# A transformer pair on one core: some chunk pairs of two down projections multiplied with seven block products in place of eight

## The chip, the cores and the metric

The kernel runs on one core of one Trainium2 chip. The metric is device microseconds of one execution. TensorE (PE in the rows, its weight loads PEld) multiplies; VectorE (DVE) and ScalarE (ACT) do everything elementwise; SyncE (SP) issues nearly all transfers.

## The reference

Two blocks are applied to 256 tokens of 2048 features, all in fp32. The first has a convolution branch and an attention branch, then a feed-forward layer; the second has block attention with pooling, then a gated convolutional feed-forward layer. What the change touches are the two down projections:

```python
    u = jnp.square(jax.nn.relu(jnp.einsum('bsd,df->bsf', h, w_ff1[l])))
    x = x + jnp.einsum('bsf,fd->bsd', u, w_ff2[l])
...
    gate, val = jnp.split(y, 2, axis=-1)
    return (jax.nn.silu(gate) * val) @ w_down
```

w_ff2 is 8192 x 2048, w_down 5632 x 2048. Between them stand the final norm of the first block and the projection w_in_2 of the second.

## The kernel before

**Precision.** Each fp32 factor is split into a high part, a copy in the matmul's fp32r format, and a low part, the rest. A product is three matmuls: high by high, high by low, low by high.

**Weights.** All weights come in tiles of 512 KB: two chunks (128 rows each) by 512 columns, called units in the code. SyncE loads them in one fixed order into five buffers RAW (`load_to`). For each, ScalarE copies the high part into WH and VectorE subtracts it for the low part in WL (`split_to`); I call this a split, and its place in WH and WL, of which there are five, a slot. RAW's buffer is free when WL is made, and then the load five further on goes out. A slot is free when TensorE is through with it. The code asks for the split of tile u+4 when TensorE's matmuls of tile u have been written down:

```python
                hl_free[u] = t
                split_to(u + AHEAD)
                pump()
                pump()
```

**The order.** Each engine's instructions are written down once, by a Python program, and then run in that order. An item is one output block of 512 columns (for 16 chunks: eight tiles). `take` gives it four of the eight PSUM banks, the two halves in turn. When its matmuls are written, its evacuation, a generator, goes into a list (`later`), and each `pump` after a tile of the next item writes down one more step of it. So the evacuation of an item stands on VectorE and ScalarE between the splits of the next one. `side` gives, within an item, the half of the banks that the item itself doesn't hold, and makes TensorE wait until they are free:

```python
            s = turn[0]
            while free[s] is None:
                assert pending
                pump()
            PE.wait([free[s]])
            free[s] = None
```

`V.step` makes a VectorE operation wait for the one ahead of it; `V.do` doesn't.

**The stages that matter.** The first feed-forward layer runs in four parts (`seg` in the code; here parts 0 to 3): four items of w_ff1 (`feature_item`, 22.3 us each) make 16 chunks of u in MHL, then four items of w_ff2 (`token_item`) multiply these 16 chunks by the part's rows and add into XT, two banks an item. The evacuation of a w_ff1 item (`ff_evac`) is: a copy TA from PSUM, an addition from PSUM, a product with RB, the relu-square, and a split into MHL. In part 3 each w_ff2 item has a longer evacuation (`final_evac`): the addition into XT, squares on ScalarE, the scaling by GF, squares again; and `turn_x_item` turns the finished quarter of x back into XHL (eight small matmuls into the side banks, then ScalarE and VectorE split them), for items 0 to 2 during the next item's sixth tile, for item 3 in the first w_in_2 item. The second feed-forward layer has three parts with 12, 16 and 16 chunks (`SEGS`). A part has gate and value items of w_up, whose evacuations (`gate2_evac`, `val2_evac`) apply a convolution with eight tap operations on VectorE, and then four w_down items. The item ahead of w_down is a gate item of the next part, except in the last part, where it is a value item, whose evacuation ends with a split into MHL.

## Time and profile before

| | us |
|---|---|
| median of 3 runs | 2402.22 (2401.73 to 2403.05) |
| the profiled execution, its own time | 2401.66 |
| its span, first to last instruction | 2399.9 |
| TensorE busy | 2392.3 |
| VectorE busy | 1515.0 |
| ScalarE busy | 1168.0 |

The span is what the profiler sees of the execution; the time has 1.8 us around it. A busy TensorE is a queue of matmuls that overlap: the length of one in a row (0.39 us) is longer than the distance from one to the next, so distances count.

### The profile page before, as it was taken

Reading aid. Unit: us, or ns where it says so; the run is one execution under the profiler, and the core shown is the slowest. Engines: PE = TensorE matmul, PEld = TensorE weight load, DVE = VectorE, ACT = ScalarE, POOL = GpSimd, SP = SyncE. Lnnn points to the kernel's source line nnn. Section 1 sums busy time; section 2 is a strip of 40 time slices with the busy share of each in tenths; the row PEclk is TensorE's granted clock in tenths of the full one; section 3 lists DMA queues with packets and bytes.
Section 4 is the critical chain, followed back from the end, with each engine's and each line's share of the span. In section 5 each row is a group of like instructions: output and inputs, shape, how many; then the busy total and the mean of one; then the engine's idle time right before and its main releaser. Section 6 shows DMA issues by size and latency. Waiting matters only on the chain.

```text
span 2399.9 us, 30366 instructions
## 1 busy us (share of the span) xinstructions
PE 2392.3 (100%) x12653; PEld 2048.4 (85%) x12653; DVE 1515.0 (63%) x1536; ACT 1168.0 (49%) x1353; POOL 0.2 (0%) x4
## 2 busy tenths in 40 slices
PE   9999999999999999999999999999999999999999
PEld 8788888888888888888888888888888888888887
DVE  6575656666566466566556667855777577756774
ACT  5454454455444344344344555555555455535552
POOL 0000000000000000000000000000000000000000
PEclk9999999999999999999999999999999999999999
DMA  7556556565556665665655565555565665566564
GB/s 251 160 178 197 165 189 196 193 188 197 186 177 203 194 220 193 194 191 190 194 188 182 188 186 164 167 183 185 185 185 196 189 192 177 202 193 187 181 208 143
DMA packets 238037, 452.13 MB, mean 188 GB/s; under 512 B 16569, under 2 KB 20779, under 8 KB 237771
## 3 DMA queue, kind: packets, MB, share of 16 engines
q1 hardware_dynamic: 237147, 449.07, 58.7%
q8 instruction: 99, 1.62, 0.3%
q10 hardware_dynamic: 752, 1.12, 0.1%
q14 instruction: 39, 0.32, 0.0%
HBM read 446.46 MB, written 3.67 MB: 188 GB/s over the span
## 4 chain that ended last, share of the span: by engine, by line
PE 99%; DVE 1%; ACT 0%; DMA 0%; issue 0%; ACTq 0%; DVEq 0%
PE PS L71 99%; DVE WL L71 0%; DMA VR<-in_g_mix 0%; DVE PB L71 0%; DVE TA L71 0%; ACT TA L71 0%; ACT WH L71 0%; DVE SEL L71 0%; DVE NC L71 0%; ACT XHL L71 0%; DVE XHL L71 0%; DVE XT L71 0%; DVE CR L71 0%; DVE SQ L71 0%; ACT CR L71 0%
## 5 line engine op out<-in xcount | busy, mean ns | idle before, releaser
L71 DVE TENSOR_TENSOR WL<-RAW,WH 128x1024 fp32r<-128x1024 f32 (+1 forms) x844 | 1021.9, 1221 | 745.9 <-ACT WH L71 745.6
L71 ACT ACTIVATE WH<-RAW 128x1024 fp32r<-128x1024 f32 (+1 forms) x845 | 881.6, 1054 | 901.7 <-PE PS L71 885.9
L71 PE MATMUL PS<-XHL,WH 128*128 128x512 f32 x3984 | 1252.9, 396 | 1.8 <-DVE CR L71 1.3
L71 PEld LDWEIGHTS PS<-XHL,WL 128*128 128x128 f32 x3968 | 745.4, 188 | 176.1
L71 PE MATMUL PS<-XHL,WL 128*128 128x256 f32 x3968 | 779.6, 278 | 0.0
L71 PE MATMUL PS<-WH,MHL 128*128 128x512 f32 x2240 | 694.1, 390 | 0.0
L71 PEld LDWEIGHTS PS<-XHL,WH 128*128 128x128 f32 x3984 | 606.5, 188 | 6.1 <-DVE CR L71 1.5
L71 PEld LDWEIGHTS PS<-WH,MHL 128*128 128x128 f32 x2240 | 420.4, 188 | 87.1
L71 PE MATMUL PS<-WL,MHL 128*128 128x512 f32 x1120 | 435.8, 389 | 0.0
L71 PEld LDWEIGHTS PS<-WL,MHL 128*128 128x128 f32 x1120 | 210.3, 188 | 42.9
L71 DVE TENSOR_TENSOR TA<-TA,PS 128x1024 f32<-128x1024 f32 x72 | 87.9, 1221 | 9.0 <-ACT TA L71 1.8
L71 ACT ACTIVATE MHL<-TA 128x1024 fp32r<-128x1024 f32 x33 | 35.0, 1061 | 116.5 <-DVE TA L71 116.5
L71 ACT COPY TA<-PS 128x1024 f32<-128x1024 f32 x72 | 73.2, 1017 | 19.7 <-DVE PB L71 3.5
L71 PE MATMUL PS<-WH,XHL 128*128 128x512 f32 x256 | 80.6, 391 | 0.1
L71 PEld LDWEIGHTS PS<-WH,XHL 128*128 128x128 f32 x256 | 48.1, 188 | 10.4 <-DVE TA L71 0.6
L71 DVE TENSOR_TENSOR MHL<-TA,MHL 128x1024 fp32r<-128x1024 f32 x33 | 40.5, 1226 | 25.3 <-ACT MHL L71 23.7
L71 DVE SCALAR_TENSOR_TENSOR TB<-TC,VEC,TB 128x256 f32<-128x256 f32 x104 | 43.2, 478 | 11.2 <-ACT TB L71 11.2
L71 PE MATMUL PS<-WL,XHL 128*128 128x512 f32 x128 | 49.9, 389 | 0.0
L71 DVE TENSOR_TENSOR XT<-XT,PS 128x1024 f32<-128x1024 f32 (+1 forms) x36 | 39.7, 1103 | 14.1 <-PE PS L71 10.5
L71 DVE SCALAR_TENSOR_TENSOR TA<-TC,VEC,TA 128x256 f32<-128x256 f32 x88 | 36.7, 478 | 11.2 <-ACT TA L71 11.2
L71 ACT ACTIVATE SQ<-XT 128x512 f32<-128x512 f32 x32 | 20.2, 632 | 43.4 <-DVE XT L71 42.9
L71 PE MATMUL PS<-AHL,WH 128*128 128x512 f32 x128 | 40.2, 395 | 0.0
(129 smaller groups left out, 785.9 us busy)
## 6 DMA issues: line engine op xcount, KB each, us to landing
RAW<-in_w_ff SPq DMA_DIRECT2D x256, 512.0 KB, 3.7
RAW<-in_w_in SPq DMA_DIRECT2D x224, 512.0 KB, 3.9
RAW<-in_w_up SPq DMA_DIRECT2D x176, 512.0 KB, 4.0
RAW<-in_w_down SPq DMA_DIRECT2D x88, 512.0 KB, 4.3
RAW<-in_w_mix_out SPq DMA_DIRECT2D x32, 512.0 KB, 3.9
RAW<-in_w_out SPq DMA_DIRECT2D x32, 512.0 KB, 3.7
RAW<-in_w_conv_out SPq DMA_DIRECT2D x16, 512.0 KB, 3.7
RAW<-in_w_attn_out SPq DMA_DIRECT2D x16, 512.0 KB, 4.4
```

The source lines that it names most:

```text
L71: ins = step[1](*step[2], **step[3])
```

## The change

Two neighbouring chunks, the two halves of the 256 tokens and two blocks of 512 columns form a 2 x 2 by 2 x 2 block product: A11, A12, A21, A22 (tokens by chunk) with B11, B12, B21, B22 (chunk by columns). It needs eight block products, of three matmuls each. For two of the pairs in each part, the second and the fourth, it is made with seven (Strassen's scheme in Winograd's form). `SEVEN` names them: two of eight pairs where a part has 16 chunks, two of six where it has 12.

- The four items of 512 columns become two `group_item`s of 1024, which hold four banks each. A normal pair is two tiles as before, with the columns side by side.
- A seven-product pair has four entries in WH and WL in place of two: `left` (B11 and B21 as loaded), `t13` and `t24` (sums of weight blocks, in T13 and T24, which lie in PB and PT) and `b22` (half a tile). VectorE makes the four sums of 512 columns: the two of T13 are written behind the split of the entry two places ahead of `left`, the two of T24 behind that of the entry just ahead of it.
- The sums of x for these pairs (S1 to S4, tiles AS, AXH, AXL) are made once a part, behind the MHL split of the w_ff1 or value item that has the chunks (`sums_x`).
- Four of the seven products are gathered over both pairs in the four side banks, and added into XT in a chain of eight operations of 512 columns, with one ScalarE copy (`sevens_evac`). Three go into the item's own banks.
- In part 3 of w_ff2 a group's two halves are evacuated one after the other with `final_evac`. Quarters 0 and 1 of x are turned back after the last two pairs of group 1, quarters 2 and 3 after the third and fourth tile of the first w_in_2 item.

```diff
+SEVEN = {8: (1, 3), 6: (1, 3)}
...
+        T13 = PB[:].rearrange("p a b -> p (a b)")[:, 0:1024]
+        T24 = PT[:].rearrange("p a b -> p (a b)")[:, 0:1024]
...
+        def sums13(u):
+
+            a, b = u % NR, (u + 1) % NR
+            left = RAW[:, a, 0:512], RAW[:, b, 0:512]
+            for i in range(2):
+                v = V.step(tt, T13[:, 512 * i:512 * i + 512], RAW[:, b, 512 * i:512 * i + 512], left[i], sub,
+                           after=[landed(u), landed(u + 1), t_free[0]])
+            return v
+
+        def sums24(u):
+
+            a, b = u % NR, (u + 1) % NR
+            V.step(tt, T24[:, 0:512], RAW[:, b, 512:1024], T13[:, 0:512], sub)
+            t_made[u] = V.step(tt, T24[:, 512:1024], RAW[:, a, 512:1024], T24[:, 0:512], sub)
...
+                t = A.do(act, hi, raw, AF.Copy, after=at + [hl_free.get(i - NS)])
                 t = V.do(tt, lo, raw, hi.bitcast(f32), sub, after=[t])
-                split_done[i] = raw_free[i] = t
-                load_to(i + NR)
+                split_done[i] = t
+                if what == "t24":
+                    t_free[0] = t
+                if done is not None:
+                    raw_free[done] = t
+                    load_to(done + NR)
                 state["split"] += 1
+                if i + 2 < len(ents) and ents[i + 2][0] == "left":
+                    sums13(ents[i + 2][1])
+                if i + 1 < len(ents) and ents[i + 1][0] == "left":
+                    sums24(ents[i + 1][1])
...
+        def group_item(steps, src, tok, stok, mid=(), tail=False):
...
+                    if n == sevens[0]:
+                        sp, bp = side()
+                    i = sevens.index(n)
+                    o, c = n == sevens[0], n == sevens[-1]
+                    PE.wait([need(i, stok), need(kcs[0], tok), need(kcs[1], tok)])
...
+                    for work in (((bp, a11, 0, o, c), (b, a12, 1, False, False)),
+                                 ((bp + 3, s1, 0, o, c), (bp + 2, s3, 1, o, c)),
+                                 ((bp + 1, s2, 0, o, c), (b + 1, a22, 1, False, False)),
+                                 ((b + 2, s4, 0, False, False),)):
+                        split_to(e)
+                        PE.wait([split_done[e]])
+                        h, l = wview(WH, e), wview(WL, e)
+                        for bank, x, k, first, last in work:
+                            t = three(bank, *x, h[:, k, :], l[:, k, :], first, last, True)
+                        hl_free[e] = t
+                        split_to(e + AHEAD)
+                        pump()
+                        e += 1
+                    ax_free[i] = t
+                    if c:
+                        later(sevens_evac(sp, bp, t, steps[0]))
...
+        def sevens_evac(s, b, t, step):
...
+            a = A.step(nc.scalar.copy, p1, PS[:, b, :], after=[t, evac_done[0]])
+            V.step(tt, x11, x11, p1, add, after=[a])
+            yield
+            V.step(tt, p16, p1, PS[:, b + 1, :], add, after=[t])
+            yield
+            V.step(tt, x12, x12, p16, add)
+            yield
+            V.step(tt, p1, p16, PS[:, b + 2, :], add)
+            yield
+            V.step(tt, x21, x21, p1, add)
+            yield
+            V.step(tt, x22, x22, p1, add)
+            yield
+            V.step(tt, x12, x12, PS[:, b + 3, :], add)
+            yield
+            free[s] = [V.step(tt, x22, x22, PS[:, b + 3, :], add)]
+            yield
...
-                mid = {}
-                if seg == 3 and g:
-                    mid = {5: [lambda: turn_x_item(g - 1, G_AT2, nxt)]}
-                it = token_item(stream(io["w_ff2"][0], 2048 * seg, ALLK, 512 * g, 512, 2), MHL, utok, 512, mid)
-                later(final_evac(it, g) if seg == 3 else residual_evac(it, g))
+                mid = {6: [lambda: turn_x_item(0, G_AT2, nxt)], 7: [lambda: turn_x_item(1, G_AT2, nxt)]}
+                it = group_item(group(io["w_ff2"][0], 2048 * seg, ALLK, g), MHL, utok, stok,
+                                mid if seg == 3 and g else {})
+                if seg == 3:
+                    later(final_evac(it, 2 * g))
+                    later(final_evac(it, 2 * g + 1))
+                else:
+                    later(group_evac(it, g))
...
-        it = w2_item(0, {3: [lambda: turn_x_item(3, G_AT2, nxt)], 5: [norm2_columns]})
+        it = w2_item(0, {2: [lambda: turn_x_item(2, G_AT2, nxt)], 3: [lambda: turn_x_item(3, G_AT2, nxt)], 5: [norm2_columns]})
```

The instructions move as follows, at three places. The first is VectorE where the first w_down item of part 0 starts, before: the evacuation of a gate item (TA, TC, the taps into TB, the last product) between the splits WL.

```order
L71 TENSOR_TENSOR TA<-TA,PS 128x1024
L71 TENSOR_TENSOR TC<-TA,RB 128x4x256
L71 TENSOR_TENSOR WL<-RAW,WH 128x1024
L71 SCALAR_TENSOR_TENSOR TB<-TC,VEC,TB 128x256 x4
L71 TENSOR_TENSOR WL<-RAW,WH 128x1024
L71 SCALAR_TENSOR_TENSOR TB<-TC,VEC,TB 128x256 x4
L71 TENSOR_TENSOR TB<-TB,TA 128x4x256
L71 TENSOR_TENSOR WL<-RAW,WH 128x1024 x4
```

The same place in the changed kernel; PB and PT are the sums T13 and T24.

```order
L72 TENSOR_TENSOR TA<-TA,PS 128x1024
L72 TENSOR_TENSOR TC<-TA,RB 128x4x256
L72 TENSOR_TENSOR WL<-RAW,WH 128x512
L72 SCALAR_TENSOR_TENSOR TB<-TC,VEC,TB 128x256 x4
L72 TENSOR_TENSOR WL<-RAW,WH 128x1024
L72 TENSOR_TENSOR PB<-RAW 128x512 x2
L72 SCALAR_TENSOR_TENSOR TB<-TC,VEC,TB 128x256 x4
L72 TENSOR_TENSOR WL<-RAW,WH 128x1024
L72 TENSOR_TENSOR PT<-RAW,PB 128x512
L72 TENSOR_TENSOR PT<-RAW,PT 128x512
L72 TENSOR_TENSOR TB<-TB,TA 128x4x256
L72 TENSOR_TENSOR WL<-RAW,WH 128x1024
```

The split behind the taps now has two sums ahead of it, and the one behind the last product two more.

The second place is VectorE between group 0 and group 1 of that part, in the changed kernel. The five splits in the first row are those of the last four tiles of group 0 and of the first of group 1; EV holds the running product sums, XT is x.

```order
L72 TENSOR_TENSOR WL<-RAW,WH 128x1024 x5
L72 TENSOR_TENSOR PB<-RAW 128x512 x2
L72 TENSOR_TENSOR XT<-XT,EV 128x512
L72 TENSOR_TENSOR EV<-EV,PS 128x512
L72 TENSOR_TENSOR WL<-RAW,WH 128x1024
L72 TENSOR_TENSOR PT<-RAW,PB 128x512
...
L72 TENSOR_TENSOR WL<-RAW,WH 128x1024
L72 TENSOR_TENSOR XT<-XT,EV 128x512 x2
L72 TENSOR_TENSOR WL<-PB,WH 128x1024
L72 TENSOR_TENSOR XT<-XT,PS 128x512 x2
L72 TENSOR_TENSOR WL<-PT,WH 128x1024
L72 TENSOR_TENSOR XT<-XT,PS 128x2x512 x2
```

Before, six splits and one addition stood there for each item. The additions XT<-XT,PS of 128x512 are the last of the product evacuation; the first matmul of group 1 waits for them.

The third place is VectorE from the end of w_ff2's part 3 into w_in_2, before: one evacuation (addition, scaling by GF) and one turning (XHL) an item.

```order
L71 TENSOR_TENSOR XT<-XT,PS 128x2x512
L71 TENSOR_TENSOR WL<-RAW,WH 128x1024
L71 TENSOR_TENSOR XT<-XT,GF 128x2x512
L71 TENSOR_TENSOR WL<-RAW,WH 128x1024 x3
L71 SCALAR_TENSOR_TENSOR XHL<-PS,VEC,XHL 128x256 x4
```

The same in the changed kernel, after the last product of group 1.

```order
L72 TENSOR_TENSOR XT<-XT,PS 128x2x512
L72 TENSOR_TENSOR WL<-RAW,WH 128x1024
L72 TENSOR_TENSOR XT<-XT,GF 128x2x512
L72 TENSOR_TENSOR WL<-RAW,WH 128x1024
L72 TENSOR_TENSOR XT<-XT,PS 128x2x512
L72 TENSOR_TENSOR WL<-RAW,WH 128x1024
L72 TENSOR_TENSOR XT<-XT,GF 128x2x512
L72 SCALAR_TENSOR_TENSOR XHL<-PS,VEC,XHL 128x256 x4
L72 TENSOR_TENSOR WL<-RAW,WH 128x1024
L72 SCALAR_TENSOR_TENSOR XHL<-PS,VEC,XHL 128x256 x4
```

Two evacuations stand one behind the other, and two turnings behind both.

## Rows read from the trace of the kernel before

**Rows 1.** Page, sections 1 and 2: busy time, and tenths in 40 slices.
```profile
PE 2392.3 (100%) x12653; PEld 2048.4 (85%) x12653; DVE 1515.0 (63%) x1536; ACT 1168.0 (49%) x1353; POOL 0.2 (0%) x4
...
PEclk9999999999999999999999999999999999999999
```

**Rows 2.** Page, section 4: the chain that ended last, shares by engine.
```profile
PE 99%; DVE 1%; ACT 0%; DMA 0%; issue 0%; ACTq 0%; DVEq 0%
```

**Rows 3.** Chain of waits: who waited for whom, us in total, times, longest.
```profile
ACT WH L71 <- PE PS L71: 885.9, 607, 5.4
DVE WL L71 <- ACT WH L71: 745.6, 553, 3.6
...
PE PS L71 <- DVE CR L71: 1.3, 1, 1.3
```

**Rows 4.** Groups by shape: busy us, mean ns of one, idle before.
```profile
L71 DVE TENSOR_TENSOR WL<-RAW,WH 128x1024 fp32r<-128x1024 f32 x840 | 1019.2, 1223 | 742.1 <-ACT WH L71 741.8
...
L71 DVE TENSOR_TENSOR XT<-XT,PS 128x512 f32<-128x512 f32 x8 | 5.5, 689 | 11.2 <-PE PS L71 10.5
...
L71 DVE TENSOR_TENSOR WL<-RAW,WH 128x512 fp32r<-128x512 f32 x4 | 2.8, 688 | 3.8 <-ACT WH L71 3.8
```

**Rows 5.** Busy time in a stretch: the four w_ff2 items of one part.
```profile
752.65:839.70 87.05, 87.05 (x386) 72.08 (x385) 47.52 (x39) 35.79 (x34) 0.00 (x0) 1.00 0.60 194
```

**Rows 6.** Timeline inside that stretch: start us, length us, instruction.
```profile
834.05 0.62 PE L71 MATMUL PS<-WH,MHL 128*128 128x512 f32 x2
...
834.50 0.39 PE L71 MATMUL PS<-WL,MHL 128*128 128x512 f32 x1
```

**Rows 7.** Timeline where the first w_ff2 item of a part starts.
```profile
752.65 0.40 PE L71 MATMUL PS<-WH,MHL 128*128 128x512 f32 x1
...
752.91 1.06 ACT L71 ACTIVATE WH<-RAW 128x1024 fp32r<-128x1024 f32 x1 [1.73 <-PE PS L71]
...
759.05 1.23 DVE L71 SCALAR_TENSOR_TENSOR TA<-TA 128x1024 f32<-128x1024 f32 x1
...
761.41 1.23 DVE L71 TENSOR_TENSOR MHL<-TA,MHL 128x1024 fp32r<-128x1024 f32 x1 [1.13 <-ACT MHL L71]
```

**Rows 8.** Timeline where the first w_down item of part 0 starts.
```profile
1822.61 0.40 PE L71 MATMUL PS<-WH,MHL 128*128 128x512 f32 x1
...
1831.51 1.22 DVE L71 TENSOR_TENSOR WL<-RAW,WH 128x1024 fp32r<-128x1024 f32 x1
...
1832.64 1.67 DVE L71 SCALAR_TENSOR_TENSOR TB<-TC,VEC,TB 128x256 f32<-128x256 f32 x4
...
1835.44 1.23 DVE L71 TENSOR_TENSOR TB<-TB,TA 128x1024 f32<-128x1024 f32 x1 [1.13 <-ACT TA L71]
```

**Rows 9.** Timeline inside w_ff2 of the last part: evacuation of a finished item.
```profile
1349.77 1.23 DVE L71 TENSOR_TENSOR WL<-RAW,WH 128x1024 fp32r<-128x1024 f32 x1 [1.50 <-ACT WH L71]
...
1351.10 1.22 DVE L71 TENSOR_TENSOR XT<-XT,PS 128x1024 f32<-128x1024 f32 x1
...
1353.74 1.04 ACT L71 ACTIVATE WH<-RAW 128x1024 fp32r<-128x1024 f32 x1
...
1356.07 1.23 DVE L71 TENSOR_TENSOR XT<-XT,GF 128x1024 f32<-128x1024 f32 x1
```

**Rows 10.** Timeline at the end of w_ff2: turning x back, first four w_in_2 tiles.
```profile
1364.74 1.03 PE L71 MATMUL PS<-CONST,XT 128*128 128x128 f32 x8
...
1365.96 1.56 ACT L71 ACTIVATE XHL<-PS,VEC 128x256 fp32r<-128x256 f32 x4
...
1367.23 1.66 DVE L71 SCALAR_TENSOR_TENSOR XHL<-PS,VEC,XHL 128x256 fp32r<-128x256 f32 x4
...
1371.07 0.62 PE L71 MATMUL PS<-XHL,WH 128*128 128x512 f32 x2
...
1382.21 1.04 PE L71 MATMUL PS<-CONST,XT 128*128 128x128 f32 x8
```

**Rows 11.** DMA issues: count, KB each, median us from issue to landing.
```profile
RAW<-in_w_down SPq DMA_DIRECT2D x88, 512.0 KB, 4.3
```

More of the change, by code:

```diff
@@ L183, in stream, with pairs @@
                     made[key].append((len(units) - 1, kcs[i:i + per]))
+                    ent_of[len(units) - 1] = len(ents)
+                    ents.append(("unit", len(units) - 1))
+            return made[key]
+        def pairs(w, row0, kcs, col0):
+            key = (w.tensor.name, w.offset, row0, tuple(kcs), col0, "pairs")
+            if key not in made:
+                made[key] = steps = []
+                for n in range(len(kcs) // 2):
+                    first = len(units)
+                    for half in range(2):
+                        r, c = row0 + 2 * n * P, col0 + 512 * half
+                        units.append((w[r:r + 2 * P, c:c + 512].rearrange("(k p) n -> p k n", p=P), 2, 512))
+                    seven = n in SEVEN[len(kcs) // 2]
+                    steps.append((seven, len(ents), kcs[2 * n:2 * n + 2]))
+                    if seven:
+                        ents.extend((what, first) for what in ("left", "t13", "t24", "b22"))
+                    else:
+                        ents.extend(("unit", first + half) for half in range(2))
             return made[key]
@@ L208, in weight_order @@
                     put(io["w_ff1"][0], k16, 2048 * seg + 512 * g)
-                for g in range(4):
-                    put(io["w_ff2"][0], k16, 512 * g, 2048 * seg)
+                for g in range(2):
+                    pairs(io["w_ff2"][0], 2048 * seg, k16, 1024 * g)
             for c in (0, 1024, 512, 1536, 3072, 3584):
@@ new lines, in three @@
+        def three(bank, xh, xl, h, l, first, last, inc):
+            PE.do(mm, PS[:, bank, :], xh, h, start=first, stop=False, inc=False)
+            PE.do(mm, PS[:, bank, :], xh, l, start=False, stop=False, inc=False)
+            return PE.do(mm, PS[:, bank, :], xl, h, start=False, stop=last, inc=inc)
+        ax_free = {}
+        group_col = {}
+        def sevens_evac(s, b, t, step):
+            c = group_col[id(step)]
+            x11, x12, x21, x22 = (XT[:, tb, c + 512 * half:c + 512 * half + 512] for tb in range(2) for half in range(2))
+            p1, p16 = EV[:, 0, :], EV[:, 1, :]
+            a = A.step(nc.scalar.copy, p1, PS[:, b, :], after=[t, evac_done[0]])
[15 more added lines that the diff above has]
+            yield
@@ new lines, in sums_x @@
+        def sums_x(seven, j, tok, after):
+            a11, a21, a12, a22 = (TA[:, j + i, tb * P:(tb + 1) * P] for i in range(2) for tb in range(2))
+            V.step(tt, AS[:, 0, :], a21, a22, add, after=after)
+            V.step(tt, AS[:, 1, :], AS[:, 0, :], a11, sub)
+            V.step(tt, AS[:, 2, :], a11, a21, sub)
+            v = V.step(tt, AS[:, 3, :], a12, AS[:, 1, :], sub)
+            a = A.step(act, AXH[:, seven], AS[:], AF.Copy, after=[v, ax_free.get(seven)])
+            tok[seven] = V.step(tt, AXL[:, seven], AS[:], AXH[:, seven].bitcast(f32), sub, after=[a])
@@ L425, in fold, with group @@
+        def group(w, row0, kcs, g):
+            steps = pairs(w, row0, kcs, 1024 * g)
+            group_col[id(steps[0])] = 1024 * g
+            return steps
         def fold(s, b, t):
@@ L951, in build, with group_evac, sevens_x, ff_evac @@
             later(residual_evac(it, g, "sum"))
-        def ff_evac(it, g, r, tok, fresh):
+        def group_evac(it, g):
+            s, b, ends = it
+            for half in range(2):
+                x4 = XT[:, :, 1024 * g + 512 * half:1024 * g + 512 * half + 512]
+                v = V.step(tt, x4, x4, PS[:, b + 2 * half:b + 2 * half + 2, :], add, after=ends[half])
+                if half == 1:
+                    free[s] = [v]
+                yield
+        def sevens_x(half_seg, n, tok, after):
+            for i, pair in enumerate(SEVEN[n]):
+                if pair // 2 == half_seg:
+                    sums_x(i, 2 * (pair % 2), tok, after)
+                    yield
+        def ff_evac(it, g, r, tok, fresh, stok):
             v = yield from fold_scaled(it, r, fresh)
@@ L957, in ff_evac @@
             split4(MHL, 4 * g, [v], tok)
+            yield
+            yield from sevens_x(g, 8, stok, [v])
         def final_evac(it, g):
-            s, b, t = it
+            s, b, ends = it
+            half = g % 2
             x4 = XT[:, :, 512 * g:512 * g + 512]
-            v = V.step(tt, x4, x4, PS[:, b:b + 2, :], add, after=[t])
-            free[s] = [v]
+            v = V.step(tt, x4, x4, PS[:, b + 2 * half:b + 2 * half + 2, :], add, after=ends[half])
+            if half == 1:
+                free[s] = [v]
             yield
@@ L1191, in val2_evac @@
             split4(MHL, c0, [v], tok)
+            yield
+            yield from sevens_x(c0 // 4, n, stok, [v])
         def out_evac(it, g):
[L1195 to L1199 removed]
+            s, b, ends = it
+            for half in range(2):
+                c = 1024 * g + 512 * half
+                for tb, (q, eng) in enumerate(((A, nc.scalar), (SP, nc.sync))):
+                    o = XT[:, tb, c:c + 512]
+                    v = V.step(tt, o, o, PS[:, b + 2 * half + tb, :], add, after=[ends[half][tb]])
+                    q.dma(eng.dma_start, io["out"][0][tb * P:(tb + 1) * P, c:c + 512], o, s_out[tb], after=[v])
+                yield
             free[s] = [v]
@@ L1203, in build @@
         utoks = [{} for _ in SEGS]
+        stoks = [{} for _ in SEGS]
         for what, si, g in FFN2:
```

111 lines of the change are left out of this document (82 added, 29 removed).

## The prediction, made before the change was run

> **What bounds the kernel now.** I read the page's busy times first. TensorE is busy for 2392.3 of 2399.9 us, VectorE for 63% and ScalarE for 49%; the clock stays in the top tenth throughout [rows 1]. The chain that ended last is TensorE for 99% [rows 2]. In the chain of waits ScalarE waits for TensorE and VectorE for ScalarE, while TensorE's longest wait in the whole run is 1.3 us [rows 3]. So a matmul removed is worth its spacing, as long as the other engines stay ahead. One part of w_ff2 has 384 matmuls of 512 columns in 87.05 us [rows 5]: 0.2267 us each, 2.72 us for a tile of twelve. w_down has the same form.
>
> **What is removed.** A seven-product pair has 21 matmuls where the pair of tiles had 24. There are 16 such pairs in w_ff2 (4 parts, 2 groups, 2 pairs) and 12 in w_down: 84 matmuls, 84 x 0.2267 = 19.0 us. All other matmuls stay, and so do the loads' number and order on SyncE's queue; a pair's two buffers are only freed later.
>
> **What is added.** A seven-product pair lasts 21 x 0.2267 = 4.76 us on TensorE. VectorE splits three whole entries at 1.22 us and half a one at 0.69 [rows 4], and makes four half-width sums at about 0.69 (the nearest row, the 128x512 subtraction): 7.1 us, where two tiles had 2.45. Over a group of 16 chunks VectorE has 12 x 1.22 + 2 x 7.1 + 8 x 0.69 for the product evacuation + 2.4 for the other + 4.9 for the evacuation of the item ahead = 41.5 us, against 12 x 2.72 + 2 x 4.76 = 42.2 on TensorE. VectorE would be nearly full, and its order is fixed, so what counts is what is late at four places. I give times from a group's first matmul (+). A half-width operation that waits for the one ahead starts 0.72 after it; splits in a row follow at 1.16; TensorE needs its data 0.23 early, for the weight load. Five slots mean that an entry's split can start only when the entry five before it is multiplied.
>
> **A. First group of each part of w_ff2.** The evacuation of the last w_ff1 item now runs in the same microseconds. In the trace its relu-square starts at +6.40 and the MHL split ends at +9.99 [rows 7]. The split ahead of the relu is now half (0.54 less), so MHL ends at 9.45 and the entry after it, the first tile of the third pair, is ready at 10.6. TensorE wants it at 2 x 2.72 + 4.76 - 0.23 = 9.97: it waits 0.66. From there the sums for the next pair end in time by 0.1 to 0.4. Four times: 2.6; in part 2 the mask addition to BIAS stands ahead and delays the chain by some 0.65. A = 3.3, bounds 0 and 7 (if each of the following splits is late too).
>
> **D. First group of each part of w_down.** The evacuation ahead has eight tap operations. In the trace the split of that same third-pair tile ends at +10.12 and the second four taps follow at once [rows 8]. TensorE waits 0.2. Now two sums stand between (1.5 us), so the next tile's split, behind the taps, is ready at 14.34 instead of 12.5; TensorE, at 10.4 + 2.72 - 0.23 = 12.9, waits 1.5. Then two sums, and the product of gate and TA (TB<-TB,TA), stand ahead of the next entry: ready at 18.3 for 17.1, so 1.2 more. 2.9 us in parts 0 and 1. In part 2 the last evacuation is that of a value item, which ends with an MHL split (1.16) ahead of T13's: another 1.0. D = 2.9 + 2.9 + 3.9 = 9.7, bounds 5 and 12.
>
> **E. From group to group in part 0 of w_down.** It has 12 chunks, so after its second seven-product pair only four tiles remain, 10.9 us. TensorE may start group 1 only when the bank additions of the products are through (the same banks). In VectorE's order there stand, ahead of the last of these, from the first sum of the next pair: four sums, eight evacuation operations and three splits, 12 x 0.72 + 3 x 1.16 + 0.3 = 12.4 us. The first sum can start 3.1 after the seventh product (its slot, ScalarE's copy, the split behind a neighbour), but it also waits for the pair's second tile, whose buffer is freed only 1.25 after that product, and 4.3 from issue to landing [rows 11] makes 5.6. So 5.6 + 12.4 - 10.9 + 0.23 = 7.4 us of waiting; without the landing 4.9. The same handover into w_up, without sums, costs 1.7: the last split ahead can start 2.72 before the end, and two additions follow. E = 9.1, bounds 4 and 10. With 16 chunks two more tiles remain, and it is through 9 us early.
>
> **B. Second group of the last part of w_ff2.** Its products need the banks of the first group. Elsewhere two additions in a row free them at +5.17, for a need at 5.21. Here the first half's whole evacuation stands ahead of the second addition: in the trace the addition follows 1.33 after its split, ScalarE is through with the two squares 1.4 after the addition, and the scaling by GF stands behind one more split [rows 9]. From the split at +1.35 that makes: addition to 3.9, squares to 5.3, the half split to 6.7, scaling to 7.95, second addition to 9.2. TensorE waits 9.2 - 5.2 = 4.0; bounds 3 and 5. In the last part of w_down, where four half-width additions stand there, it is 0.4.
>
> **C. From w_ff2 into w_in_2.** Before, x is turned back a quarter at a time inside four items. Now two quarters are turned inside group 1 and two inside the next item. First, the second turning is the last thing in the group and uses the banks that the next item starts with: turning 1.03, ScalarE 1.56, VectorE's last half 0.83 [rows 10] make 3.5, less 0.85 of turning, plus 0.23: 2.9 us. Second, the third turning stands after three tiles, 3 x 2.785 = 8.4 (four tiles from 1371.07 to 1382.21 [rows 10]), and needs the other group's banks, freed by the fourth quarter's addition, which stands behind the third quarter's addition, squares, scaling and squares: addition at 1.05, scaling done 7.3, a split behind 1.4 of squares to 11.0, addition to 12.4. 4.3 us. Third, the fourth turning needs the third's banks: squares, scaling, squares to 16.5, ScalarE 1.56, VectorE to 19.05, for a need at 16.1: 3.0. C = 10.2, bounds 6 and 12.
>
> **The sum.** Waits 3.3 + 9.7 + 9.1 + 4.0 + 0.4 + 10.2 = 36.7; less 19.0 is +17.7. The profiled execution took 2401.66 (2399.9 of span and 1.8 around it), 0.6 below the median of 2402.22, so 2419.4: I say 2419. The sums of x are made in 14 items of w_ff1 and w_up, six operations of at most 0.72 each; behind the 22.3 us of an item's eight tiles, with VectorE half idle, I take them as hidden, and without that cover they cost up to 60. The end is the same addition and store.
>
> In the trace the matmul that ends a tile raises the semaphore, and the next follow at the usual distance: 0.45 us for two, as anywhere [rows 6]. The Trainium skill (TensorE: Matmul & The Clock Gate, The cost: per-tile semaphore tail) counts 26.3 ns for each increment, here 140 more in the seven-product pairs and 160 in the other tiles of these items, which would add 7.9 us, and by that alone the sum would be 2427. The trace shows none of it, and I take 0.
>
> **The rivals.** *The banks are free in time*: B, C and E cost nothing, the rest stays. 2401.7 - 19.0 + 3.3 + 9.7 = 2395.7. For it speaks that TensorE never waited for banks before; against it, that these waits are read off a fixed order, each with several microseconds to spare. It decides below 19 us of waits in all. *VectorE keeps up everywhere*, as the 37% idle might suggest: 2383 to 2386; against it, 7.1 us for 4.76. *The clock falls*: five waits of 2.9 to 7.4 us are longer than any before, under which the granted clock stayed 1.00, its 2.4 GHz level [rows 1, 3]. At 1.2 GHz each matmul costs another 0.2267; with ten to twelve after each such wait the time is 2431 to 2433. The Trainium skill (TensorE: Matmul & The Clock Gate, Part 1) says that idleness lowers the clock; no run here shows it yet. That the change does nothing is excluded: its order has 84 matmuls fewer.
>
> **The numbers.** Waits as worked out 0.62; clock 0.12; banks free 0.14; VectorE keeps up 0.08; in between 0.04. By the bounds of A to E the first reaches from 2401 to 2429; that all five lie at their low ends at once is unlikely, so its own range is 2404 to 2429. The clock's case makes the top 2433, and 8 in 10 is only reached by taking in half of the banks' case, so the low end is 2397; VectorE keeping up is left out. Within 0.2% is about what can be told from no change, 2397.4 to 2407.0. Banks free lies at its lower edge, so I halve it, and the case in between too: faster 0.07 + 0.08 + 0.02 = 0.17, the same 0.07 + 0.02 and 0.01 of the first case's low end, 0.10, slower 0.73.
>
> **What would show it.** TensorE's waits for VectorE, near zero before, should be near 37 us in all, longest (7 us) at the start of the second group of w_down's part 0, released by an addition into XT; three at the end of w_ff2 of 3 to 4 us; one to two us in w_down's first groups before WL. A sum of waits under 14 us would make the forecast's sign wrong; a granted clock under 1.00 behind the long waits would speak for the third rival.

## The result and the profile after

The changed kernel takes 2426.52 us (median; 2424.52 to 2427.43), before 2402.07. The ratio is 1.0100, 95% interval 1.0082 to 1.0117: slower by 24.4 us. The profiled execution has a span of 2422.7 us, 22.8 more than before, and with the 1.8 around it 2424.5.

The page of the changed kernel, its busy times, TensorE's 40 slices and the shares of the chain that ended last ([rows 1, 2] are the same before):

```profile
PE 2383.5 (98%) x12569; PEld 2035.3 (84%) x12569; DVE 1734.6 (72%) x1886; ACT 1225.2 (51%) x1437; POOL 0.2 (0%) x4
...
PE   9999999999999999999999899999998999999999
...
PE 91%; DVE 6%; ACT 1%; DMA 0%; issue 0%; DVEq 0%; ACTq 0%
```

TensorE has 84 matmuls fewer and is busy for 8.8 us less, VectorE is busy for 219.6 us more and is still free for 28% of the time. Two of TensorE's slices, the 23rd and the 31st, have fallen to 8: the end of w_ff2, and the first part of w_down. What TensorE waited for, in all, times, longest; before, its longest wait was 1.3 us [rows 3]:

```profile
PE PS L72 <- DVE XT L72: 17.0, 4, 8.4
PE PS L72 <- DVE WL L72: 9.2, 11, 1.3
PE PS L72 <- DVE XHL L72: 5.4, 2, 2.8
```

These 31.6 us are new. In distances between matmuls (which also count the refilling of the queue) they are 34.4 us. TensorE's rows at the waits of the predicted places B, C (three) and D (two), each with its wait in brackets:

```profile
1328.22 0.80 PE L72 MATMUL PS<-WH,MHL 128*128 128x512 f32 x1 [4.14 <-DVE XT L72]
...
1371.07 0.73 PE L72 MATMUL PS<-XHL,WH 128*128 128x512 f32 x2 [2.62 <-DVE XHL L72]
...
1384.42 0.44 PE L72 MATMUL PS<-CONST,XT 128*128 128x128 f32 x2 [3.15 <-DVE XT L72]
...
1391.12 0.55 PE L72 MATMUL PS<-CONST,XT 128*128 128x128 f32 x3 [2.83 <-DVE XHL L72]
...
1845.96 0.50 PE L72 MATMUL PS<-WH,MHL 128*128 128x512 f32 x1 [1.24 <-DVE WL L72]
...
1849.89 0.50 PE L72 MATMUL PS<-WH,MHL 128*128 128x512 f32 x1 [0.89 <-DVE WL L72]
```

The longest wait is E, at the start of group 1 in the part of 12 chunks. The chain that ended last, followed there (start, length, what):

```profile
1848.69 7.43 DVE WL L72 x7
...
1856.14 5.71 DMA RAW<-in_w_down
...
1861.92 0.70 DVE PB L72
...
1863.45 0.70 DVE XT L72
...
1864.24 0.69 DVE EV L72
1864.93 1.15 DVE WL L72
...
1866.10 0.70 DVE PT L72
...
1873.44 0.70 DVE XT L72
...
1874.19 2.07 PE PS L72 x4
```

It reads as the prediction wrote it down: the last split that frees a buffer, the load of the next pair's second tile, T13's first sum, and then the product evacuation with splits and sums between its steps, until the last addition lets TensorE go on at 1874.19.

One thing more than waits is in the trace. Busy times by stretch of the changed kernel; the column behind POOL is the granted clock:

```profile
1328.20:1331.20 3.00, 2.98 (x7) 2.42 (x8) 2.10 (x3) 2.15 (x5) 0.00 (x0) 0.50 0.01 2
...
1372.30:1375.60 3.30, 3.30 (x12) 2.80 (x12) 1.22 (x1) 1.44 (x4) 0.00 (x0) 0.50 0.55 156
...
1384.40:1391.00 6.60, 3.88 (x24) 3.33 (x24) 3.92 (x6) 5.25 (x13) 0.00 (x0) 1.00 0.49 152
...
1870.70:1877.30 6.60, 3.11 (x7) 2.48 (x8) 6.23 (x8) 0.00 (x0) 0.00 (x0) 0.50 0.24 79
1877.50:1900.00 22.50, 22.50 (x101) 18.60 (x100) 17.06 (x18) 12.91 (x14) 0.00 (x0) 1.00 0.55 176
```

Behind B (seven matmuls in 3.00 us), behind the first wait of C and behind E (seven in 3.11 us) TensorE ran at 0.50, its 1.2 GHz level; behind the second wait of C, and up to the third, it did not (1384.40). Half of 3.0, 3.3 and 3.1 us is lost: 4.7 us. So the account is 34.4 of waits and 4.7 of clock, less 19.0, or +20.1; the span grew by 22.8. Of the other 2.7 us, 1.6 stand right behind the waits: in 14 places at full clock the second matmul starts 0.34 us after the first in place of 0.23. The rest, 1.1 us, I can't assign. The sums of x cost nothing, as forecast: the four w_ff1 items of part 1 take 89.05 us from first to last matmul before and after. The median lies another 2.0 us above the profiled execution; the granted clock of the other three runs was 0.995 to 0.996 in place of 0.997, which is 4.8 to 9.7 us more at half clock; what of it falls on matmuls costs half. The clocks are read to 0.001, so this is a rough figure.

### The profile page after: what moved, and what is told of

It reads as the page before. It is cut to its first block, busy times and chain, and to the rows that moved or that the text cites. A ratio compares the mean times of both kernels' runs of the same rounds, so it can differ in the third digit from the quotient of the medians.

```text
span 2422.7 us, 30747 instructions
## 1 busy us (share of the span) xinstructions
PE 2383.5 (98%) x12569; PEld 2035.3 (84%) x12569; DVE 1734.6 (72%) x1886; ACT 1225.2 (51%) x1437; POOL 0.2 (0%) x4
## 4 chain that ended last, share of the span: by engine, by line
PE 91%; DVE 6%; ACT 1%; DMA 0%; issue 0%; DVEq 0%; ACTq 0%
PE PS L72 91%; DVE WL L72 2%; DVE TA L72 1%; DVE XT L72 1%; ACT WH L72 1%; DVE TB L72 0%; DVE PB L72 0%; DVE MHL L72 0%; DMA RAW<-in_w_down 0%; DVE PT L72 0%; ACT SQ L72 0%; ACT MHL L72 0%; DVE XHL L72 0%; ACT TA L72 0%; DMA VR<-in_g_mix 0%
## 5 line engine op out<-in xcount | busy, mean ns | idle before, releaser
L72 DVE TENSOR_TENSOR WL<-RAW,WH 128x1024 fp32r<-128x1024 f32 (+1 forms) x844 | 1003.1, 1202 | 491.5 <-ACT WH L72 488.7
L72 ACT ACTIVATE WH<-RAW 128x1024 fp32r<-128x1024 f32 (+1 forms) x845 | 865.7, 1039 | 743.3 <-PE PS L72 717.6
L72 PE MATMUL PS<-WH,MHL 128*128 128x512 f32 x1960 | 621.8, 392 | 20.6 <-DVE XT L72 12.5
L72 PEld LDWEIGHTS PS<-WH,MHL 128*128 128x128 f32 x1960 | 369.2, 188 | 103.4 <-DVE XT L72 13.9
L72 PE MATMUL PS<-WL,MHL 128*128 128x512 f32 x980 | 382.5, 390 | 0.0
L72 PEld LDWEIGHTS PS<-WL,MHL 128*128 128x128 f32 x980 | 184.8, 189 | 36.9
L72 DVE TENSOR_TENSOR XT<-XT,PS 128x512 f32<-128x512 f32 (+1 forms) x64 | 59.0, 921 | 12.9 <-PE PS L72 7.4
L72 ACT ACTIVATE WH<-PB 128x1024 fp32r<-128x1024 f32 x28 | 29.7, 1060 | 62.5 <-DVE PT L72 45.9
L72 DVE TENSOR_TENSOR PB<-RAW 128x512 f32<-128x512 f32 x56 | 38.8, 693 | 13.4 <-DMA RAW<-in_w_ff 6.0
L72 DVE SCALAR_TENSOR_TENSOR TA<-TC,VEC,TA 128x256 f32<-128x256 f32 x88 | 36.7, 479 | 11.7 <-ACT TA L72 11.7
```

Source lines behind the costliest of these rows:

```text
L72: ins = step[1](*step[2], **step[3])
```

## The experiments

**The theory**: VectorE's written order makes the waits, each at its own place, and each can be removed without the others; the 19.0 us are really saved. **Rival 1**: VectorE has too much work around a product pair, so a wait removed at one place comes back at another. **Rival 2**: seven products cost TensorE more than was counted. Rival 2 falls by the trace after alone. TensorE's rows at the first use of the sums of x in the two product pairs of an undisturbed group:

```profile
802.38 0.39 PE L72 MATMUL PS<-WH,AXH 128*128 128x512 f32 x1
...
812.58 0.39 PE L72 MATMUL PS<-WH,AXH 128*128 128x512 f32 x1
```

Between them lie 45 matmuls (21 of the pair, 24 of the normal one) in 10.20 us, 0.2267 each, as [rows 5]. The Trainium skill (TensorE: Matmul & The Clock Gate, The cost: per-tile semaphore tail) would, by an estimate from its 26.3 ns, add some 0.3 us for the 11 increments in this distance; the trace shows none. That the median is near the 2427 that this rule gave is chance.

| kernel | expected | median | ratio to before, 95% |
|---|---|---|---|
| groups without products | 2412.5 | 2412.75 | 1.0029 to 1.0055 |
| no products in the part of 12 | 2413.3 | 2413.30 | 1.0030 to 1.0058 |
| last part of w_ff2 as before | 2412.0 | 2411.67 | 1.0026 to 1.0053 |
| additions first | 2415.4 | 2422.12 | 1.0067 to 1.0094 |
| pairs 2 and 4 | 2418.1 | 2424.01 | 1.0078 to 1.0106 |
| products in a row | 2417 | 2426.65 | 1.0085 to 1.0117 |
| waits alone | 2455 to 2465 | 2429.19 | 1.0093 to 1.0132 |
| combined | 2392.5 | 2393.04 | 0.9950 to 0.9976 |
| fewer steps a tile | 2389 | 2392.35 | 0.9942 to 0.9969 |
| last part in groups | 2387.5 | 2397.85 | 0.9971 to 0.9989 |
| one pair of six | 2386.5 | 2396.48 | 0.9962 to 0.9984 |
| one pair of six, last part as before | 2391.2 | 2390.45 | 0.9936 to 0.9963 |

In the numbering of `SEVEN`, which begins at 0, the changed kernel has (1, 3).

**Groups without products.**

```diff
-SEVEN = {8: (1, 3), 6: (1, 3)}
+SEVEN = {8: (), 6: ()}
```

> The changed kernel with no seven-product pair at all: items of 1024 columns, the later evacuation of w_ff2's last part and the moved turnings stay. My theory (the time is lost in waits that VectorE's written order makes, three of them at the end of w_ff2 by the groups alone): TensorE waits only at the step into w_in_2, 2.7 + 3.2 + 2.9 us, one stretch at half clock of 3.4 us behind it costs 1.7 more, and nothing else changes: 2402 + 10.5 = 2412.5 us, range 2409 to 2414. Rival 1 (VectorE simply has too much work in the product pairs, and the groups are harmless): 2402. Rival 2 (the form of the seven products costs TensorE more than counted): 2402 too.

Measured: 2412.75 us. The waits for WL are gone and B and E with them; C is left. TensorE's waits in this kernel:

```profile
PE PS L72 <- DVE XHL L72: 4.2, 3, 2.6
PE PS L72 <- DVE XT L72: 4.0, 1, 4.0
```

So 8.2 us of waits have nothing to do with the seven products: they come from items of 1024 columns and the late turning of x. The sum was right and two of its parts were not: the second and third wait are 4.0 and 1.5 us for 3.2 and 2.9, and the half clock stands behind the second wait and not behind the first.

**No products in the part of 12 chunks.**

```diff
-SEVEN = {8: (1, 3), 6: (1, 3)}
+SEVEN = {8: (1, 3), 6: ()}
```

> The changed kernel with seven products in the parts of 16 chunks alone, none in the first part of w_down. My theory: the waits of 8.5 and 1.55 us at the ends of its groups go, the 6.8 us at half clock behind the first of them (3.4 us) and the 2.45 us in its first group; 4 pairs, 2.7 us, are not saved: 2426.5 - 10.05 - 3.4 - 2.45 + 2.7 = 2413.3 us, range 2411 to 2416. Rival 1 (VectorE's amount of work): the pair's share of its work goes, a seventh of all: the 41.8 us that were lost fall by a seventh, 2426.5 - 6.0 + 2.7 = 2423.

Measured: 2413.30 us. Four product pairs alone cost 13 us by the medians. Rival 1's 2423, a ratio of 1.0087, lies outside the interval. That the figure is hit to the tenth is partly luck: it takes 3.4 us for the clock at E, where half of 3.1 is 1.6.

**The last part of w_ff2 as before.**

```diff
+                for g in range(4 if seg == 3 else 2):
+                    if seg == 3:
+                        put(io["w_ff2"][0], k16, 512 * g, 2048 * seg)
...
+                    mid = {5: [lambda: turn_x_item(g - 1, G_AT2, nxt)]} if g else {}
+                    it = token_item(stream(io["w_ff2"][0], 2048 * seg, ALLK, 512 * g, 512, 2), MHL, utok, 512, mid)
+                    later(final_evac(it, g))
```

> The changed kernel, but the last part of w_ff2 is computed as before the change: four items of 512 columns with eight products, x turned back a quarter at a time. My theory: the waits there go (4.66 at the start of its group 1, 8.8 at the step into w_in_2, 0.36 in its group 0) and the two stretches at half clock (3.4 us); 4 pairs, 2.7 us, are not saved: 2426.5 - 13.8 - 3.4 + 2.7 = 2412.0 us, range 2410 to 2415. Rival 1 (VectorE's amount of work): a seventh of it goes, and with it a seventh of the loss, 2423.

Measured: 2411.67 us. TensorE's waits:

```profile
PE PS L72 <- DVE XT L72: 10.5, 2, 9.1
PE PS L72 <- DVE WL L72: 8.6, 10, 1.3
```

Only E with its successor, and A and D, are left. Three experiments that take a place away hit their number within 0.4 us, although an interval of 0.0028 in the ratio is over 6 us wide. Their numbers are terms read off the changed kernel's trace, so what they show is that these places add up and go one by one.

**Additions first.** The next three move work and take none away. Here a group's two additions come first in w_ff2's last part:

```diff
-                    later(final_evac(it, 2 * g))
-                    later(final_evac(it, 2 * g + 1))
+                    later(final_evac(it, g))
...
+            for half in range(2):
...
+                added.append(V.step(tt, x4, x4, PS[:, b + 2 * half:b + 2 * half + 2, :], add, after=ends[half]))
...
+            for half in range(2):
...
+                a = squares(SUM1, q, 512, added[half])
```

> The changed kernel, but in the last part of w_ff2 a group's two additions from PSUM are written ahead of the squares and the scaling of either half. VectorE has exactly the same work. My theory: the wait of 4.3 us at the start of group 1 goes (0.3 left) and the half clock behind it (1.7); of the waits of 3.2 and 2.9 us in the first w_in_2 item some 0.7 is left; the 2.7 us ahead of it stay, with their half clock: 2426.5 - 4.0 - 1.7 - 5.4 = 2415.4 us, range 2413 to 2418. Rival 1 (VectorE's amount of work): the same work comes late elsewhere, and less than half of that is won: 2421 to 2426.

Measured: 2422.12 us. B went as expected (0.6 left), and so did the second wait of C. But the third grew to 5.3 us. The timeline of VectorE and ScalarE ahead of it:

```profile
1380.15 1.23 DVE L72 TENSOR_TENSOR XT<-XT,GF 128x1024 f32<-128x1024 f32 x1
1381.41 0.63 ACT L72 ACTIVATE SQ<-XT 128x512 f32<-128x512 f32 x1 [2.55 <-DVE XT L72]
...
1382.80 1.55 ACT L72 ACTIVATE XHL<-PS,VEC 128x256 fp32r<-128x256 f32 x4
1383.65 1.66 DVE L72 SCALAR_TENSOR_TENSOR XHL<-PS,VEC,XHL 128x256 fp32r<-128x256 f32 x4 [2.27 <-ACT XHL L72]
```

The third quarter of x was turned on time, but its copy out of PSUM (1382.80) stands on ScalarE behind the scaling and the squares of the fourth, and the fourth turning needs the same banks. I had moved a queue's head and not asked what then stood at its tail. VectorE was idle for 2.27 us there, so this wait is not its amount of work.

**Pairs 2 and 4.**

```diff
-SEVEN = {8: (1, 3), 6: (1, 3)}
+SEVEN = {8: (2, 4), 6: (1, 3)}
```

> The changed kernel with the third and the fifth pair of a part of 16 chunks as seven-product pairs in place of the second and the fourth; the work is the same. My theory: the sums for the second such pair then stand behind the evacuation of the item ahead, so the waits of 0.35 to 1.2 us in w_ff2's first groups (2.2 in all) and of 2.45 and 3.8 us in w_down's parts 1 and 2 go; six normal tiles, 16.3 us, still stand behind the last product, so no bank is late: 2426.5 - 8.4 = 2418.1 us, range 2415 to 2421. Rival 1 (VectorE's amount of work): no change, 2425 to 2428, as the same work meets the same evacuation. Rival 3 (the banks come free two tiles later and are late in every part): slower, above 2430.

Measured: 2424.01 us (2421.51 to 2429.36). TensorE's waits:

```profile
PE PS L72 <- DVE XT L72: 17.7, 5, 7.8
PE PS L72 <- DVE WL L72: 7.0, 6, 1.8
PE PS L72 <- DVE XHL L72: 5.0, 4, 2.6
```

Those for WL fell from 11 to 6, as the theory has it, but by 2.2 us and not by 8.4. In the last part of w_ff2 the later products hold the banks that the turnings of the first two quarters need: two new waits there. And the wait in the first group of w_ff2's part 2, where the mask addition stands, grew from 1.0 to 1.8. This counts for rival 1's side: there, waits moved.

**Products in a row.**

```diff
             V.step(tt, x11, x11, p1, add, after=[a])
-            yield
             V.step(tt, p16, p1, PS[:, b + 1, :], add, after=[t])
-            yield
...
```

> The changed kernel, but the eight additions of the product evacuation are written one right behind the other, with no split between them; the work is the same. My theory (in the first part of w_down the wait at the start of group 1 comes from what stands among these additions in VectorE's order): the banks then come free 5.6 us (landing) + 1.5 (two sums) + 5.8 (eight additions) after the last product, against 10.9 of TensorE's work: the wait of 8.5 us falls to some 2.2, that of 1.55 into w_up goes, of the half clock behind it (3.4) half is left; the splits are up to 5.8 us later, which the slots cover: 2426.5 - 7.9 - 1.7 = 2417 us, range 2414 to 2421. Rival 1 (VectorE's amount of work): no change, or new waits for WL of the same size: 2425 to 2428.

Measured: 2426.65 us, no change. E's wait fell from 8.4 to 3.6 us and that into w_up went, but waits of 1.3 us came at a second group of w_ff2, and B grew from 4.1 to 5.5. VectorE in that second group, in this kernel:

```profile
792.51 1.42 DVE L72 TENSOR_TENSOR PB<-RAW 128x512 f32<-128x512 f32 x2 [3.66 <-DMA RAW<-in_w_ff]
```

and in the changed kernel:

```profile
788.18 1.42 DVE L72 TENSOR_TENSOR PB<-RAW 128x512 f32<-128x512 f32 x2
```

I had said that the slots cover the splits being later. They do, but a later split also frees its RAW buffer later, so the load five further on goes out later (the two ahead of this sum at 785.47 and 786.61 us, in the changed kernel at 780.32 and 782.90), and T13's sum at the head of VectorE's queue waits 3.66 us for it. The clock took its share too: the stretches at 0.50 hold some 15.3 us of matmuls, in the changed kernel 9.4. Order still makes the wait, but through the loads, and a place is not free of its neighbours where the work is only moved.

By the times alone, the three runs that move work speak for rival 1: additions first and products in a row end in its ranges, 2421 to 2426 and 2425 to 2428, and pairs 2 and 4 between its range and the theory's. That each wait can be removed without the others holds where a place is taken away; it fails where work is moved. What speaks against VectorE's amount of work as the cause is in the traces, where VectorE was idle at two of these waits, and in the combined kernel below.

**Waits alone**, to price the clock by itself.

```diff
+CHAIN = {(0, 2): 1, (0, 3): 2, (1, 1): 0, (1, 2): 1, (1, 3): 4, (2, 1): 2, (2, 2): 0, (2, 3): 8,
+         (3, 1): 1, (3, 2): 4, (3, 3): 2}
...
+                if (seg, g) in CHAIN:
+                    junk = PT[:].rearrange("p a b -> p (a b)")[:, 0:512]
+                    v = V.now
+                    for i in range(CHAIN[seg, g]):
+                        v = V.step(tt, junk, junk, junk, add, after=[PE.now])
+                    PE.wait([v])
```

> The kernel before the change with eleven waits put in: at the start of an item of w_ff1 TensorE waits until VectorE has ended its last split and then 0, 1, 2, 4 or 8 additions of 512 columns on a tile that is not used there. No other work is changed. Each wait should last some 2.3 us plus 0.72 for each addition, 43 us in all. If a wait costs only its length: 2445 us, and the granted clock stays 1.00. If the clock falls behind waits, as in the changed kernel (waits of 2.7, 4.3 and 8.5 us had stretches of 3.4, 3.4 and 6.8 us at half clock behind them, those of 2.9 and 3.2 us none), another 1.7 to 5 us each behind most of them: 2455 to 2465.

Measured: 2429.19 us, from two runs that lie 4 us apart (2427.19, and the profiled one at 2431.20). I had sized the waits wrongly: the last split was already done, so each lasted about 0.74 for an addition and no more. In the chain of waits, and by stretch:

```profile
PE PS L73 <- DVE PT L73: 18.7, 9, 5.9
```

```profile
735.60:760.00 24.40, 24.40 (x137) 21.22 (x138) 15.02 (x13) 10.65 (x11) 0.00 (x0) 1.00 0.52 177
...
916.00:922.00 6.00, 5.93 (x18) 5.08 (x19) 3.59 (x4) 0.34 (x1) 0.00 (x0) 0.50 0.24 87
...
1102.90:1106.30 3.40, 3.37 (x10) 2.90 (x11) 3.26 (x3) 0.00 (x0) 0.00 (x0) 0.50 0.28 90
...
1288.40:1300.00 11.60, 11.60 (x66) 10.13 (x67) 9.40 (x8) 4.83 (x6) 0.00 (x0) 1.00 0.36 120
```

Behind the two waits of 3.0 us and that of 5.9 the clock stood at 0.50 (rows 2 and 3, and again at 1263.5); behind the six of 0.8 and 1.6 us it stayed at 1.00 (the rows of 735 and 1288 follow such waits). With no other work changed, 18.7 us of waits cost 27.0 us by the median: the clock has a price of its own behind waits, in the profiled run some 6 us (half of 6.0, 3.4 and 3.3). The other run had a mean clock of 0.999 for 0.996 and was 4 us shorter, which suggests that the same waits do not always pay it.

**Combined**: products only where the theory sees no late bank.

```diff
-SEVEN = {8: (1, 3), 6: (1, 3)}
+SEVEN = {8: (2, 4), 6: ()}
...
+                if seg == 2 and g == 2:
+                    mid = {4: [lambda: tk.update(bias=V.step(tt, BIAS[:], BIAS[:], over4(M, 8), add, after=[(s_wp, 16)]))]}
```

and the last part of w_ff2 as above.

> Seven products where the theory sees no late bank: the third and fifth pair of the parts with 16 chunks, none in the part of 12, the last part of w_ff2 as before the change, and the addition of the mask to BIAS moved from the start of w_ff2's third part into an item of w_ff1. 20 pairs x 3 matmuls x 0.2267 = 13.6 us saved. My theory: left are waits of 1.5 us in w_down's second part, 2.0 in its third and 0.4 at the end, and no stretch at half clock: 2402.15 - 13.6 + 3.9 = 2392.5 us, range 2390 to 2396, faster than both kernels. Rival 1 (VectorE's amount of work): the product pairs cost on the average what they cost in the changed kernel (24 us lost over 28 pairs, net), 2402 + 17 = 2419; at the least no faster than 2402.

Measured: 2393.04 us, ratio 0.9963. Of VectorE's waits, those for WL are all that is new:

```profile
PE PS L72 <- DVE WL L72: 2.3, 3, 1.9
```

Behind the longest of them, 1.9 us, the clock stood at 0.50 for 3.4 us, where I had expected no such stretch:

```profile
2318.70:2322.00 3.30, 3.30 (x9) 2.61 (x8) 3.23 (x5) 0.00 (x0) 0.00 (x0) 0.50 0.53 176
```

This decides against rival 1: 20 product pairs with the same work on VectorE for each, and a net gain of 9.1 us of the 13.6.

**Fewer steps a tile.**

```diff
                         pump()
-                        pump()
+                        if not slow or n > sevens[-1]:
+                            pump()
```

> The combined kernel (third and fifth pair of the parts of 16 chunks, none in the part of 12, last part of w_ff2 and the mask addition as there), and in the first group of each part only one step of the evacuation, in place of two, is written after a tile, up to the second seven-product pair. My theory: the product and the MHL split of the item ahead then stand behind the split that TensorE waits for, so of the waits of 0.3 + 0.3 and 0.4 + 2.1 us that were left in w_down's second and third part some 0.5 remains, and the stretch of 3.4 us at half clock behind the longest goes: 2393.0 - 2.6 - 1.5 = 2389 us, range 2387.5 to 2391.5; with no wait at all it would be 2388.6. If the steps only move the wait: 2392 to 2394.

Measured: 2392.35 us. The steps were only moved: the waits for WL are 2.6 us, four times, the longest 0.8, and no half clock. The two kernels can't be told apart.

**The last part in groups.** The steps of its evacuation are regrouped, and each turning has two banks of its own:

```diff
+            for q, x4, v in halves:
+                done.append(squares(SUM1, q, 512, v))
+                yield
+            for (q, x4, v), a in zip(halves, done):
+                tk["x", q] = V.step(tt, x4, x4, GF[:, None, 512 * q:512 * q + 512].to_broadcast([P, 2, 512]), mul,
...
+            s, b = hold[0] if hold else side()
+            if first:
+                hold.append((s, b + 2))
```

> The kernel with fewer steps a tile, but the last part of w_ff2 in groups with seven products again (second and fourth pair), its evacuation reordered: both additions, the squares of both halves, both scalings, the squares of the scaled halves; the first two quarters of x are turned together after the seventh pair, each in two banks of its own, and so are the last two in the first w_in_2 item. My theory: four more pairs save 2.7 us, and the waits of 4.3 and 8.8 us that this part had in the changed kernel came from the order of the steps and from the shared banks alone; left are some 1.0 at its start and at its end: 2389 - 2.7 + 1.2 = 2387.5 us, range 2386 to 2391. If the late turnings are due to VectorE's work there: 2393 to 2397.

Measured: 2397.85 us, 5.5 more than the kernel it is built on. The waits of B and of the shared banks are gone, but TensorE waits 2.3 us for the third quarter, with the clock at half behind it, 1.3 at the step into w_in_2, and several times under 1. VectorE ahead of the longest:

```profile
1373.22 1.23 DVE L73 TENSOR_TENSOR WL<-RAW,WH 128x1024 fp32r<-128x1024 f32 x1 [2.87 <-ACT WH L73]
1374.48 2.48 DVE L73 TENSOR_TENSOR XT<-XT,GF 128x1024 f32<-128x1024 f32 x2
```

ScalarE at the same time, the last of four squares and the copy behind it:

```profile
1371.52 0.64 ACT L73 ACTIVATE SQ<-XT 128x512 f32<-128x512 f32 x1
...
1372.15 1.04 ACT L73 ACTIVATE WH<-RAW 128x1024 fp32r<-128x1024 f32 x1
```

The scalings stand behind a split whose copy stands on ScalarE behind four squares. Again VectorE is idle (2.87 us, before TensorE's wait begins at 1373.5) for want of a copy, and then late. This run came out just above the other forecast's range (2393 to 2397), but the rows don't show its reason, VectorE's work.

**One pair of six**, on the last part in groups and then on the last part as before.

```diff
-SEVEN = {8: (2, 4), 6: ()}
+SEVEN = {8: (2, 4), 6: (2,)}
```

The edit does one thing more: the first group of the part of 12 also gets one evacuation step a tile in place of two, up to its product pair.

> The kernel with the last part in groups, and in the part of 12 chunks the third of six pairs with seven products in both groups. My theory: behind its products six tiles remain, 16.3 us, so no bank is late; 2 pairs save 1.4 us and the first group waits some 0.4: 1.0 less than the last part in groups, some 2386.5 us, range 2385 to 2390. If the evacuation of the products is late in this part whatever the place of the pair (the 8.5 us of the changed kernel): 2393 or more.

> The kernel with fewer steps a tile (last part of w_ff2 as before the change), and in the part of 12 chunks the third of six pairs with seven products in both groups. My theory: six tiles stand behind its products, so nothing is late, as the same edit showed on the kernel with the last part in groups (1.4 us faster); two pairs save 1.4 us and up to 0.5 is waited in the first group: 2392.35 - 1.1 = 2391.2 us, range 2390 to 2392.5, the fastest of all. If the products' evacuation is late there, one wait of TensorE of over 1 us released by an addition into XT shows in the first part of w_down, and the time is 2393 or more.

Measured: 2396.48 us, 1.4 less than its base, and 2390.45 us, the lowest of all: ratio 0.9950, 0.9936 to 0.9963. That is 1.4 less than its base by the two ratios (1.9 by the medians; the kernel before, run beside each, differs by 1.1). The first misses its range, 2385 to 2390, by what its base had missed. Both gains are near what was expected, but the intervals overlap with those of the bases, so their size is not shown. No distance between matmuls above 0.5 us is left in the first part of w_down in either: with six tiles behind the last product, the same additions are through in time. Two things changed for E at once, and the runs don't part them. Six tiles stand behind the product in place of four; and the next group's sums, which in the changed kernel stood ahead of the additions and waited for a load, stand behind them: here the additions end at 1845.1 us and the first sum starts at 1846.3. Of the second, TensorE's waits:

```profile
PE PS L72 <- DVE WL L72: 2.5, 4, 0.8
```

22 pairs save 15.0 us, these waits and their refilling take 3.2, and 11.7 were measured.

## Why the prediction was right, and where it was not

The forecast of slower, by waits that outweigh 19.0 us, was right, and every wait lay at its predicted place with its predicted releaser. By its own terms, in distances between matmuls:

| term | predicted | after |
|---|---|---|
| matmuls removed | -19.0 | -19.0 |
| A, first groups of w_ff2 | 3.3 | 2.3 |
| B and the end of w_down | 4.4 | 4.6 |
| C, into w_in_2 | 10.2 | 8.7 |
| D, first groups of w_down | 9.7 | 8.7 |
| E, part of 12 chunks | 9.1 | 10.1 |
| clock | 0 | 4.7 |

A to E sum to 34.4 for 36.7. E is larger by a landing of 5.7 us where the nearest row had 4.3; the second wait of C is 3.2 for 4.3. That the waits belong to these places is shown for B, C, E and the first part's share of D by the experiments that take the place away. For A and the rest of D it is shown only as far as the combined kernel goes, where the second pair of sums stands behind the evacuation and 2.3 us are left.

The step that failed is the clock, which the sum put at nothing and which took 4.7 us. I put its fall among the rivals at 0.12, and the likeliest case had none, on the ground that the clock had stayed at 1.00, but before there was no wait above 1.3 us to try it on. Waits of 2.6 us and more, which the forecast itself had, should have carried some of its price in the sum. The rival was too large as well: it counted five falls of 2.3 to 2.7 us, and there were three of some 1.6. With the median's 2.0 us above the profiled execution, which I read as more of the same, the clock explains most of the 7 us between 2419 and 2426.5. That it does so neatly is partly luck: the waits were 2.3 us under the forecast, and the 2.7 us outside the account nearly cancel that. Of the working, one sum is off: VectorE's work over a group of 16 chunks adds up to 41.7 us, not 41.5, and nothing rests on the difference.

What was only argued: where the last 1.1 us lie, and that the three runs not profiled here lost their 2 us to the clock at these same places.

## What to carry to other kernels

Where an engine in order serves a saturated one, a saving of work must be weighed by its late places, not by shares: 28% free on VectorE did not help, and at two of the late places in the experiments it stood idle for 2 to 3 us, during or just ahead of TensorE's wait for it. To price a change like this, write down what stands in the queue ahead of the one operation that frees a bank, a buffer or a slot, and compare it with the work that the waiting engine has left; that gave each term within 1.5 us here. A theory of such waits is best used to choose where the change is applied at all (the same block product gains 11.7 us on 22 pairs), since rewriting the order left a wait in another place in all five trials of it, through ScalarE's queue, shared banks or the load buffers.

## What the runs showed of the hardware

In the profiled executions of the changed kernel and the experiments the granted clock fell to 0.50 behind or within every wait of TensorE of 3.6 us or more (up to 9.1), behind some of those from 1.9 to 3.2 us and not behind others: at the step into w_in_2 a wait of 2.6 us had it in the changed kernel and not in groups without products. Behind waits of 1.6 us or less in w_ff1 it stayed. But behind the wait of 1.3 us at about 89 us, which every kernel here has and at which the profiles of the kernel before and of the changed kernel keep 1.00, it fell in two of the other profiled executions, no products in the part of 12 and last part in groups; the first of them:

```profile
89.30:92.60 3.30, 3.30 (x12) 2.79 (x11) 1.16 (x1) 1.05 (x2) 0.00 (x0) 0.50 0.78 249
```

So a wait's length alone didn't settle it, and some of the spread between executions has nothing to do with the change. That idleness lowers the clock is what the Trainium skill says (TensorE: Matmul & The Clock Gate, Part 1), and these rows agree: every stretch at 0.50 with matmuls in it stands behind or around a wait. Unexpected was the clock's spread: the same wait E had it at half for 3.1 us behind it in the changed kernel, and for 5.9 with additions first, which alone makes 1.4 us of difference.
